# The value projections of the gated and the retention layer with tokens on the partitions: h stationary, 256 weight columns moving, two K parts

## The reference

```python
h = rms_norm(x, norm1_g)                       # [512, 1024]
proj = h @ w_in
...
# gated linear attention, per head: q, k [512, 128], v [512, 256]
attn = sum_k q[t, k] * k[s, k] * decay[t, s, k]
o = q_t exp(bcum) @ state + attn @ v
state = exp(blast) * state + (k * exp(blast - bcum)).T @ v
...
# retention, per head: q, k [512, 128], v [512, 256]; after it a group norm over the 256 columns of a head,
# so the mean of a head's 256 values may be taken off v itself, token by token
```

## Time and profile before

| | |
|---|---|
| median of 3 runs | 2340.46 us (2340.29 to 2341.34) |
| the profiled execution, its own time | 2340.38 us |
| its span in the profile | 2338.7 us |
| TensorE matmuls, busy | 2321.0 us (99%), 14408 of them |
| VectorE busy | 1640.4 us (70%) |
| ScalarE busy | 1023.9 us (44%) |
| DMA | 206.33 MB, mean 88 GB/s |

### The profile page before, as it was taken

The page is one execution under the profiler, slowest core; times in us unless marked ns, Lnnn a source line. Parts: engine busy times, 40 slices in busy tenths (PEclk is TensorE's granted clock), DMA queues, the critical chain, the costliest instruction groups (busy, mean ns, idle before and its releaser), DMA issues.

```text
span 2338.7 us, 35336 instructions
## 1 busy us (share of the span) xinstructions
PE 2321.0 (99%) x14408; PEld 1955.9 (84%) x14408; DVE 1640.4 (70%) x2344; ACT 1023.9 (44%) x1511; POOL 150.0 (6%) x172
## 2 busy tenths in 40 slices
PE   9999999999999999999999999999999999999999
PEld 7877778787888999877778999988888888899998
DVE  7666656888668777676658877766755556787774
ACT  5444463447254343356656333443423223634332
POOL 5111110000000000042120000000000000100000
PEclk9999999999999999999999999999999999999999
DMA  4222213222323333321123333322222212333321
GB/s 161 75 72 66 73 47 108 82 73 71 101 90 109 101 106 109 108 72 51 32 84 107 109 100 100 107 82 91 74 71 82 90 55 66 114 111 108 109 92 71
DMA packets 60675, 206.33 MB, mean 88 GB/s; under 512 B 7249, under 2 KB 7249, under 8 KB 60386
## 3 DMA queue, kind: packets, MB, share of 16 engines
q1 hardware_dynamic: 59760, 202.93, 27.9%
q10 hardware_dynamic: 754, 1.14, 0.2%
HBM read 201.94 MB, written 2.10 MB: 87 GB/s over the span
## 4 chain that ended last, share of the span: by engine, by line
PE 54%; DVE 1%; ACT 1%; issue 0%; DVEq 0%; ACTq 0%
PE psum L1977 22%; PE psum L2393 5%; PE psum L2392 5%; PE psum L2391 5%; PE psum L2348 4%; PE psum L2350 4%; PE psum L2349 4%; PE psum L2142 1%; PE psum L2038 1%; PE psum L2095 1%; PE psum L2045 1%; PE psum L2055 0%; PE psum L2051 0%; PE psum L2113 0%; PE psum L2004 0%; PE psum L2023 0%
## 5 line engine op out<-in xcount | busy, mean ns | idle before, releaser
L770 ACT CAST whi<-raw 128x1024 fp32r<-128x1024 f32 (+1 forms) x399 | 400.0, 1005 | 471.4 <-PE psum L2393 195.0
L1180 DVE TENSOR_TENSOR wlo<-raw,whi 128x1024 fp32r<-128x1024 f32 (+1 forms) x399 | 466.3, 1169 | 31.5 <-ACT whi L770 30.7
L1977 PE MATMUL psum<-hhi,whi 128*128 128x512 f32 x872 | 346.9, 398 | 5.0 <-DVE wlo L1180 2.8
L1977 PE MATMUL psum<-hlo,whi 128*128 128x512 f32 x872 | 344.8, 395 | 0.0
L1977 PE MATMUL psum<-hhi,wlo 128*128 128x512 f32 x872 | 342.6, 393 | 0.0
L2393 PE MATMUL psum<-hhi,wlo 128*128 128x512 f32 x768 | 299.6, 390 | 0.0
L2392 PE MATMUL psum<-hlo,whi 128*128 128x512 f32 x768 | 299.5, 390 | 0.0
L2391 PE MATMUL psum<-hhi,whi 128*128 128x512 f32 x768 | 299.0, 389 | 0.0
L1977 PE MATMUL psum<-uhi,whi 128*128 128x512 f32 x624 | 247.5, 397 | 0.0
L1977 PE MATMUL psum<-ulo,whi 128*128 128x512 f32 x624 | 245.6, 394 | 0.0
L1977 PE MATMUL psum<-uhi,wlo 128*128 128x512 f32 x624 | 244.3, 392 | 0.0
(11 more groups left out here) (311 smaller groups left out, 4266.7 us busy)
## 6 DMA issues: line engine op xcount, KB each, us to landing
raw<-in_packed_dram SPq DMA_DIRECT2D x359, 512.0 KB, 3.5
raw<-in_packed_dram SPq DMA_DIRECT2D x40, 256.0 KB, 2.6
x<-in_xt_dram SPq DMA_DIRECT2D x8, 256.0 KB, 5.1
out_dram<-x SPq DMA_DIRECT2D x8, 256.0 KB, 2.0
arena<-in_near_bias_dram ACTq DMA_DIRECT2D x1, 1024.0 KB, 6.1
vec<-in_vec_dram ACTq DMA_DIRECT2D x1, 44.0 KB, 3.9
arena<-in_gla_gate_up_dram ACTq DMA_DIRECT2D x1, 32.0 KB
arena<-in_gla_gate_bias_dram ACTq DMA_DIRECT2D x1, 2.0 KB
```

The costliest lines, as they stand in the source:

```text
L770: nc.scalar.copy(whi[:, u % 4, 0:kt, :], raw[:, u % 4, 0:kt, :]).then_inc(hi_done, 1)
L1180: dve.tensor_tensor(wlo[:, u % 4, 0:kt, :], raw[:, u % 4, 0:kt, :], whi[:, u % 4, 0:kt, :].bitcast(F32), ALU.subtract).then_inc(lo_done, 1)
L1977: mm = pe.matmul(g, w[:, u % 4, k, :], v[:, k, :], start=n == 0, stop=n == 3 * kt - 1)
```

## The change

The two `turn` units of a head's values become a pair of `rows` units. Both cover all 256 columns of the head and all 512 tokens, the first over K 0 to 511, the second over K 512 to 1023; each is still 512 KB of weights. In `row_products` the activations are the stationary operand (128 tokens by 128 features of `hhi`, `hlo` or `uhi`, `ulo`) and 256 weight columns move: 4 token blocks x 4 K tiles x 3 products = 48 matmuls a unit. The sum stays open over the pair: tokens 0 to 255 in `XB`, tokens 256 to 511 in the bank of the unit's partner (`row_banks`). Values come out with tokens on partitions, so the transposes go. `rstd` is then needed per partition: `columns(i)` transposes it once a layer (4 transposes and a 128x4 copy into `rstd_rows`). VectorE reads each pair once (`evacuate_rows`, two operations of 128x512), in the retention layer it then takes off the mean in place (`centre_rows`, one sum and one subtraction over 128x1024). `begin` has new rules: the first unit of a pair waits for the previous pair's `XB`; before its matmul 24, where it moves to the second bank, it waits until that bank's last user, the k unit just before it, has been posted; and the second `silu` unit waits for the pair's `posted`.

```diff
-                + [("turn", w, 0, VG + 2 * P * h + P * i, KD, ("g", h, i)) for i in range(2)]
+                + [("rows", w, D // 2 * i, VG + 2 * P * h, KD, ("g", h, i)) for i in range(2)]
...
-                + [("turn", w, 0, 2 * D + 2 * P * h + P * i, KD, (h, i)) for i in range(2)]
+                + [("rows", w, D // 2 * i, 2 * D + 2 * P * h, KD, ("r", h, i)) for i in range(2)]
...
+        rstd_rows = sb("rstd_rows", [P, 2, NT])
         with nc.sbuf_tensor("arena", [P, 17000], F32) as arena:
...
+        def row_banks(u):
+
+            return XB, psum[:, (u if ROWU[u] % 2 else u + 1) % 2, :]
...
+            def evacuate_rows(u):
+
+                v, stage_at = row_values(u), 0 if units[u][5][0] == "g" else 1
+                dve.wait_ge(rstd_columns, stage_at + 1)
+                for i, g in enumerate(row_banks(u)):
+                    dve.wait_ge(unit_done, DONE[u] + 1)
+                    r = rstd_rows[:, stage_at, 2 * i:2 * i + 2].rearrange("p (t c) -> p t c", c=1).to_broadcast([P, 2, 2 * P])
+                    ins = dve.tensor_tensor(v[:, 2 * i:2 * i + 2, :], g.rearrange("p (t c) -> p t c", t=2), r, ALU.mult)
...
+            def centre_rows(u):
+
+                v = row_values(u)
+                dve.wait_ge(posted, u)
+                dve.tensor_reduce(r_mean, v, AX.X, ALU.add).then_inc(dve_step, 1)
+                dve.wait_ge(dve_step, chain.up())
+                dve.tensor_scalar(r_mean, r_mean, 1.0 / (2 * P), None, ALU.mult).then_inc(dve_step, 1)
+                dve.wait_ge(dve_step, chain.up())
+                mean = r_mean.rearrange("p (t c) -> p t c", c=1).to_broadcast([P, NT, 2 * P])
+                dve.tensor_tensor(v, v, mean, ALU.subtract).then_inc(posted, 1)
...
+            def row_products(u, n0, n1, hi, lo):
+
+                half = ROWU[u] % 2
+                for n in range(n0, n1):
+                    t, k, part = n // 12, n // 3 % 4, n % 3
+                    if half == 0 and n == 24:
+                        bank_free(u - 1)
+                    g = row_banks(u)[t // 2][:, 2 * P * (t % 2):2 * P * (t % 2) + 2 * P]
+                    v, w = ((hi, whi), (lo, whi), (hi, wlo))[part]
+                    mm = pe.matmul(g, v[:, 4 * half + k, P * t:P * t + P],
+                                   w[:, u % 4, 2 * k:2 * k + 2, :].rearrange("p k c -> p (k c)"),
+                                   start=half == 0 and n % 24 == 0, stop=half == 1 and n % 24 == 23)
...
             def begin(u):
                 pe.wait_ge(lo_done, u + 1)
+                if u in ROWU:
+                    if ROWU[u] % 2 == 0:
+                        which, h, _ = units[u][5]
+                        if h:
+                            pe.wait_ge(posted, row_unit(which, h - 1) + 1)
+                        elif which == "g":
+                            pe.wait_ge(rstd_columns, 1)
+                        else:
+                            pe.wait_ge(posted, first("l3"))
+                    return
                 if u >= 2:
 
-                    if u - 2 in EVACU:
-                        pe.wait_ge(evacuated, EVACU[u - 2] + 1)
-                    else:
-                        pe.wait_ge(posted, u - 1)
+                    bank_free(u - 4 if u - 2 in ROWU and ROWU[u - 2] % 2 == 0 else u - 2)
+
+            def columns(i):
+
+                if i == 0:
+                    pe.wait_ge(posted, UNIT_OF["turn", "w_in", 0, 4096 + 3 * P] + 1)
+                pe.wait_ge(norm_rstd, ORDER["l3" if i else "l1"] + 1)
+                for t in range(NT):
+                    mm = pe.transpose(columns_bank(i)[:, P * t:P * t + P], rstd[:, P * t:P * t + P], ident[:, :])
+                mm.then_inc(rstd_turned, 1)
```

More of the change, by code:

```diff
@@ L184, in head @@
         return ([("copy", w, 0, P * h, KD, ("q", h)), ("copy", w, 0, D + P * h, KD, ("k", h))]
-                + [("turn", w, 0, 2 * D + 2 * P * h + P * i, KD, (h, i)) for i in range(2)]
+                + [("rows", w, D // 2 * i, 2 * D + 2 * P * h, KD, ("r", h, i)) for i in range(2)]
                 + [("silu", w, 0, 4 * D + 2 * P * h + P * i, KD, (h, i)) for i in range(2)])
     ret = [[("ret", h, i) for i in range(6)] for h in range(HEADS)]
-    todo = list(zip(head(0), [None] + [("rates", i) for i in range(4)] + [None]))
+    todo = list(zip(head(0), [None, ("rates", 0), [("columns", 1), ("rates", 1)], ("rates", 2), ("rates", 3), None]))
     for h in range(1, 5):
@@ L494, in build, with row_unit, columns_bank @@
         GATEU = {u: i for i, u in enumerate(u for u, s in enumerate(units) if s[0] in GATES)}
+        ROWU = {u: i for i, u in enumerate(u for u, s in enumerate(units) if s[0] == "rows")}
+        rstd_turned, rstd_columns = sem("rstd_turned"), sem("rstd_columns")
+        def row_unit(which, h, half=0):
+            name, col = ("w_in", VG) if which == "g" else ("w_in_o_2", 2 * D)
+            return UNIT_OF["rows", name, D // 2 * half, col + 2 * P * h]
+        def row_banks(u):
+            return XB, psum[:, (u if ROWU[u] % 2 else u + 1) % 2, :]
+        def columns_bank(i):
+            return psum[:, 2, :] if i else XB
         EVACU = {u: i for i, u in enumerate(u for u, s in enumerate(units) if s[0] in ("turn", "head", "up") + GATES)}
@@ L979, in nothing @@
                 pass
-            PARTS = {"ret": ret, "rates": rates, "att": att, "bias": nothing, "lg": lg, "gla": gla, "sums": nothing, "pa": pa, "mask": nothing}
+            PARTS = {"ret": ret, "rates": rates, "att": att, "bias": nothing, "lg": lg, "gla": gla, "sums": nothing, "pa": pa, "mask": nothing,
+                     "columns": nothing}
             def static(name):
@@ L1228, in post @@
                 kind, _, _, _, _, j = units[u]
+                if kind == "rows":
+                    if j[0] == "r" and j[2] == 1:
+                        centre_rows(u)
+                    return
                 g, s = psum[:, u % 2, :], stage[:, u % 2, :]
@@ L1660, in bias @@
                 dve.wait_ge(dve_step, chain.up())
-            PARTS = {"ret": ret, "rates": rates, "att": att, "bias": bias, "lg": lg, "gla": gla, "mask": mask, "sums": sums, "pa": pa}
+            PARTS = {"ret": ret, "rates": rates, "att": att, "bias": bias, "lg": lg, "gla": gla, "mask": mask, "sums": sums, "pa": pa,
+                     "columns": columns}
             def static(name):
@@ L1957, in products @@
                 kt = units[u][4]
+                if u in ROWU:
+                    row_products(u, n0, n1, hi, lo)
+                    return
                 g = bank(u)
@@ L2017, in ret @@
                 if part == 0:
-                    pe.wait_ge(posted, UNIT_OF["turn", "w_in_o_2", 0, 2 * D + 2 * P * h + P] + 1)
+                    pe.wait_ge(posted, row_unit("r", h, 1) + 1)
                     if h:
@@ L2205, in gla @@
                 if part == 2:
-                    pe.wait_ge(posted, UNIT_OF["turn", "w_in", 0, VG + 2 * P * h + P] + 1)
+                    pe.wait_ge(posted, row_unit("g", h, 1) + 1)
                     if h:
@@ L2250, in _ @@
             PARTS = {"ret": ret, "rates": nothing, "att": att, "bias": nothing, "lg": lg, "gla": gla, "sums": nothing, "pa": nothing, "mask": mask, "norm": lambda n: norm(n),
+                     "columns": columns,
                      "shared_bank": shared_bank}
@@ L2272, in static @@
                         begin(u)
-                        total = 3 * units[u][4]
+                        total = 48 if u in ROWU else 3 * units[u][4]
                         k0 = units[u][2] % D // P
@@ L2432 @@
             w = flat[name][row:row + 4 * P, col:col + 2 * P].reshape(4, P, 2, P).transpose(2, 0, 1, 3).reshape(kt, P, P)
+        elif kind == "rows":
+            w = flat[name][row:row + 4 * P, col:col + 2 * P].reshape(4, P, 2 * P)
         else:
```

47 lines of the change are left out of this document (25 added, 22 removed).

## The result

| | before | after |
|---|---|---|
| median of 11 runs each | 2340.41 us (2338.86 to 2341.79) | 2346.1 us (2344.14 to 2348.36) |
| ratio | | 1.0025, 95% interval 1.0017 to 1.0032 |
| profiled execution, own time | 2340.38 us | 2345.12 us |
| its span | 2338.7 us | 2343.4 us |

The change costs 5.7 us. 2338.8 was forecast, with 2345.5 as the upper end: the kernel is slower, and by 0.6 us outside the range of 2333.0 to 2345.5.

A forecast was written before the change was run, and what follows sets the result against it. TensorE's instruction stream, busy 99% of the span, was taken to bound the kernel. Transposes -10.8, narrower matmuls +5.4 and two waits +3.8 sum to -1.6 us on 2340.4, so 2338.8 us, range 2333.0 to 2345.5.

The forecast's parts named there:

- Transposes: TensorE's value units in both layers: 22 fewer blocks of four transposes at 0.49 us each, 10.8 us less.
- Narrower matmuls: Value units: 1152 matmuls of 256 columns at 118 ns replace 576 of 512, 5.4 us more, ends 0 and 7.7.
- rival of a fast stream: Value units' narrow matmuls run at 113.3 ns, 2333.4 us; or the two waits go, 2335.0; both, 2329.6; chance 0.27.
- estimate from the Trainium skill: Narrow matmuls: 262 cycles for 256 columns against 518 for 512, +1.5 us, giving an estimated 2334.9.
- New wait before matmul 24: Gated attention, heads 2 and 3: TensorE waits 1.9 us each for VectorE to post the k unit, 3.8 us more.
- nothing else gets late behind it: Behind the waits at matmul 24, VectorE and ScalarE catch up: no further loss, but no time given back.
- Second gate unit and centring: Retention layer: pair posted at 5.5 us, TensorE arrives at 5.9 (even in heads 0 and 5), so no cost.
- slower rival: Retention centring too late: sum over 128x1024 takes twice 1.2 us, second gate units wait, 7.4 us, 2346.2; chance 0.13.
- The MLPs as long as before: MLP stages, with their 39 seven-product groups, were expected not to change in time.
- Moved data: `rstd_rows` shifts the arena 32 bytes; if rates hang on addresses, MLP groups change 6.2 us either way (2345.0 if slower); chance 0.08.
- forecast's own range: Main case's span, 2335.5 to 2341.5 us: stream at 115 to 120 ns, waits 1.5 to 2.2 us each; chance 0.52.

The follow-up runs named there:

- e3: e2 with the last part of the head before (`out`) moved one unit later, behind the post of the k unit; 2335.32 us, ratio 0.9977.
- e8: The kernel before, transposes kept, with each matmul of the 24 value units split in two of 256 token columns; 2346.36 us, ratio 1.0028.
- e2: The changed kernel with `rstd_rows` allocated behind `cols`, so the arena lies where it lay before; 2342.57 us, ratio 1.0008.
- e1: The kernel before with 32 unused bytes ahead of the arena and nothing else; 2344.01 us, ratio 1.0015.
- e4: The kernel before with the 64 bytes of `nbias` moved between `wlo` and `hhi`, the arena unmoved; 2352.48 us, ratio 1.0050.
- e6: e3 with 32 bytes (`const`) put between the weights' and the activations' tiles; 2365.3 us in one run.

## Why the prediction was wrong

By its own steps:

- **Transposes, -10.8.** Right. 24 blocks went and 2 came; the profiles of e3 and e8 together put one at 0.48 us.
- **Narrower matmuls, +5.4 with ends 0 and 7.7.** Mis-sized: undisturbed stretches run at 120 ns, the upper end, +7.7; over both layers, interruptions and all, the width cost 6.6 us in e8's profile and +6.3 in its time. The prediction took 118 because it could not say what decides between 113 and 120. The runs now show one thing that does: how `whi` and `hhi` lie to each other. At the distance of this kernel it is 120; at 64 bytes more, 114 in undisturbed stretches. The rival of a fast stream, at 113.3 ns, is out for this kernel. The estimate from the Trainium skill (TensorE: Matmul & The Clock Gate, Back-to-back issue gap), 262 cycles a matmul or +1.5 us, disagrees with the trace of after, which has 120 ns (11.52 us for 96); the measurement decides.
- **New wait before matmul 24, +3.8.** Right in place, number and size (1.9 us lost from 456.13 to 458.16), and in the heads that it spares. What failed is the sentence that nothing else gets late behind it. The granted clock fell after it, in one head of two in the profiled execution of after and in both in that of e2: +5.4 and +6.9 in place of 3.8. The prediction had only rows in which TensorE's waits were rare, and the earlier trace rows hide, in a slice of 58 us, the fall to 0.59 that before itself has behind a wait of 2.0 us, from 1052 to 1056.
- **Second gate unit and centring, nothing.** Right. First gate unit of a retention head at 1637.96, `wlo` from 1639.55, sum over 128x1024 from 1640.69 in 1.21 us, subtraction from 1642.14 in 1.22, so the pair is posted 5.4 us in, where 5.5 was forecast and 5.9 allowed (timeline of DVE after). The slower rival fell at the point that it named, a sum that scales as all else.
- **The MLPs as long as before.** This is the step that failed and put the result outside the range. *Moved data* had a chance of 0.08 against it, on the ground that nothing in the trace tied a rate to an address. The rival was true: 39 x 0.08 to 0.1 us, +3.1 to +3.8 (e1: 3.6, e2: 3.5). And the trace did hold the hint, twice. First, one instruction form, in one stream, without waits, ran at two steady rates in seven products that differ only in which tiles they read. The prediction saw this, called the cause unknown, and then treated it as unlikely to move. Second, the same holds for the wide matmuls, which it did not look at: in the timeline of PE before, 24 that move `hhi` take 5.44 us, 226.7 ns each, and the 33 right behind them that move `blocks`, in the arena, 7.70 us, 233.3 each.

```profile
664.12 0.39 PE L1977 MATMUL psum<-hhi,whi 128*128 128x512 f32 x1
...
669.56 0.63 PE L1977 MATMUL psum<-blocks,whi 128*128 128x512 f32 x2
...
677.26 0.39 PE L2330 MATMUL psum<-hhi,ones_r 128*128 128x512 f32 x1
```

The sum with the terms put right: -10.8 + 7.7 + 5.4 + 3.8 = +6.1, or 2346.5 on the profiled 2340.4; the median of after is 2346.1. That the two are so close is in part luck: the layers gave -4.0 and not -3.1 for the first two terms, which makes +5.2, and the clock adds more or less from one execution to the next. Against the -1.6 of the forecast 7.7 us are missing: 3.8 of moved data, 2.3 of the narrow rate, 1.6 of clock. Each is as large as the net effect forecast; a sum of opposed terms of 5 to 10 us leaves no room for one left out. (The forecast's own range is also summed a microsecond too high at its lower end: with 115 ns and 1.5 us a wait it is 2334.5, not 2335.5.)

What stays open: which property of the distance sets the rate (32 and 128 bytes slow the wide stream more than 64 does, which no rule of these runs explains), what else chooses between 229 and 233 ns at 64 bytes, and why the clock fell behind some waits of 1.75 to 2 us and not behind others.

## What to carry to other kernels

In a stream of matmuls with no waits, the distance between starts is a measured thing, and it can change by 3% when unrelated data moves: allocate a new small tensor behind everything that TensorE reads, or compare with a version padded in the same way before judging a change of half a per cent. A wait put into a full TensorE stream can cost more than its length, since the clock may fall behind it (2.0 us without a fall, 3.4 with one); here moving one part of VectorE's work by one unit turned a loss of 5.7 us (with the data put back) into a gain of 5.1, and e3_out_later is the version to keep.

## What the runs showed of the hardware

- The rate of fp32r matmuls depends on how the tile that moves lies in SBUF to the one that stands. With 0 or 768 bytes between them added, 226.5 to 226.7 ns for 512 columns and 120 for 256; with 64, 229.0 and 114 (but 233.3 in a stream of e4); with 32, 233.1 and 118; with 128, 232.3 and 119. 32 unused bytes ahead of the arena cost this kernel 3.6 us (e1); 32 between the weights and the activations cost e3 30.0 (e6, one run).
- At each of the three distances that slowed the wide matmuls of these stretches (32, 64, 128 bytes), the narrow ones of the value units got 1 to 6 ns quicker.
- Behind a wait of TensorE of 1.75 us the granted clock was 0.55 and 0.59 in two windows of 2 us, near the lower of its two levels, 1.2 GHz, and that head took 1.4 us longer than the other; behind the other's wait, of the same length in the same execution, it stayed at 1.00.
- A matmul stream split into twice as many of half the width, with a weight load each, was 6.3 us slower over 1152 narrow matmuls (e8).
